# A two-block transformer kernel: where the modulation rows are placed in the first half

## The reference, cut to what matters

```python
mod = silu(c) @ w_ada[l] + b_ada[l]                 # 1024 x 6144
sh_m, sc_m, gt_m, sh_f, sc_f, gt_f = split(mod, 6)
h = rms_norm(x, g_pre_mix[l]) * (1 + sc_m) + sh_m
y = token_mixer(h, ...)                              # 3656 columns of w_in, attention, w_out
x = x + gt_m * rms_norm(y, g_post_mix[l])
h = rms_norm(x, g_pre_ffn[l]) * (1 + sc_f) + sh_f
y = (gelu(conv3(h @ w_up_act)) * (h @ w_up_lin)) @ w_down     # width 2816
x = x + gt_f * rms_norm(y, g_post_ffn[l])
```

## Time and profile before

| what | value |
|---|---|
| median of 3 runs | 2878.32 us (2877.91 to 2879.34) |
| the profiled execution | 2881.45 us, its span 2879.8 us |
| mean granted clock of TensorE | 0.937 of full speed |
| TensorE matmul busy | 2512.0 us (87%) |
| VectorE busy | 1790.6 us (62%) |
| ScalarE busy | 1218.0 us (42%) |
| GpSimd busy | 1000.2 us (35%) |
| bytes moved | 412.98 MB, 143 GB/s on average |
| first network (to the first block of columns of the second) | about 960 us |

### The profile page before, as it was taken

The page is one execution under the profiler, slowest core; times in us unless marked ns, Lnnn a source line. Parts: engine busy times, 40 slices in busy tenths (PEclk is TensorE's granted clock), DMA queues, the critical chain, the costliest instruction groups (busy, mean ns, idle before and its releaser), DMA issues. The chain is left out here.

```text
span 2879.8 us, 34433 instructions
## 1 busy us (share of the span) xinstructions
PE 2512.0 (87%) x12828; PEld 2073.3 (72%) x12828; DVE 1790.6 (62%) x2311; ACT 1218.0 (42%) x2102; POOL 1000.2 (35%) x827
## 2 busy tenths in 40 slices
PE   2986978986969799998775899999899997999898
PEld 2765976765867678886442778888788886777897
DVE  5777686875668687775997544454554534245554
ACT  3434444445555443445443433233433334234543
POOL 0111100113355687771554345443353421001221
PEclk9997999997989899999887999999899998999999
DMA  8445576443455355553100133344233332221452
GB/s 297 154 154 208 201 263 224 154 152 126 183 210 214 132 172 182 195 167 125 41 32 15 52 139 146 117 147 153 81 132 140 144 126 88 88 92 56 143 194 96
DMA packets 118294, 412.98 MB, mean 143 GB/s; under 512 B 13552, under 2 KB 17776, under 8 KB 118128
## 3 DMA queue, kind: packets, MB, share of 16 engines
q1 hardware_dynamic: 117152, 407.49, 40.5%
q10 hardware_dynamic: 976, 3.29, 0.3%
HBM read 409.68 MB, written 1.05 MB: 143 GB/s over the span
## 5 line engine op out<-in xcount | busy, mean ns | idle before, releaser
L1581 DVE TENSOR_TENSOR sl<-raw,sh 128x1024 fp32r<-128x1024 f32 x534 | 757.0, 1441 | 518.6 <-ACT sh L1272 518.3
L1006 PE MATMUL ps<-hH,sh 128*128 128x256 f32 (+1 forms) x2496 | 844.0, 338 | 81.3 <-DVE hL L1667 61.8
L1007 PE MATMUL ps<-hL,sh 128*128 128x256 f32 (+1 forms) x2496 | 838.1, 336 | 0.0
L1008 PE MATMUL ps<-hH,sl 128*128 128x256 f32 (+1 forms) x2496 | 837.4, 336 | 0.0
L1272 ACT ACTIVATE sh<-raw 128x1024 fp32r<-128x1024 f32 x534 | 539.5, 1036 | 341.0 <-PE ps L1008 300.7
L1006 PEld LDWEIGHTS ps<-hH,sh 128*128 128x128 f32 x2496 | 484.4, 194 | 139.8 <-issue 52.4
L1007 PEld LDWEIGHTS ps<-hL,sh 128*128 128x128 f32 x2496 | 483.4, 194 | 51.9 <-issue 1.0
L1008 PEld LDWEIGHTS ps<-hH,sl 128*128 128x128 f32 x2496 | 483.3, 194 | 51.4
L2054 POOL TENSOR_TENSOR raw<-raw,cB 128x1024 f32<-128x1024 f32 x144 | 375.8, 2610 | 185.3 <-DVE V L1593 182.9
L1593 DVE CUSTOM_DVE_ANT_0 mjunk<-raw,cB,V 128x1024 bf16<-128x1024 f32 x240 | 382.0, 1592 | 31.8 <-DMA V<-in_vec 16.4
L2125 POOL TENSOR_TENSOR uLl<-F,uHh 128x256 fp32r<-128x256 f32 (+1 forms) x132 | 156.7, 1187 | 565.7 <-ACT uHh L1468 442.5
(11 more groups left out here) (183 smaller groups left out, 2719.8 us busy)
## 6 DMA issues: line engine op xcount, KB each, us to landing
raw<-in_w SPq DMA_DIRECT2D x756, 512.0 KB, 4.3
raw<-in_w SPq DMA_DIRECT2D x16, 256.0 KB, 3.1
cB<-in_rpb SPq DMA_DIRECT2D x64, 64.0 KB, 2.6
X<-in_x ACTq DMA_DIRECT2D x1, 1024.0 KB, 12.1
X<-in_ctx ACTq DMA_DIRECT2D x1, 1024.0 KB, 18.5
out<-X SPq DMA_DIRECT2D x2, 512.0 KB, 3.1
raw<-in_w SPq DMA_DIRECT2D x2, 288.0 KB, 4.6
cB<-in_c ACTq DMA_DIRECT2D x1, 512.0 KB, 6.0
```

The source lines that it names most:

```text
L1006: self.e.matmul(out, lh, rh, start=start, stop=False)
L1007: self.e.matmul(out, lh, rl, start=False, stop=False)
L1008: return self.e.matmul(out, ll, rh, start=False, stop=stop)
L1581: self.e.tensor_tensor(lo[:, 0:w], raw[:, 0:w], hi[:, 0:w].bitcast(F32), ALU.subtract).then_inc(self.sems["w_lo"], 1)
```

## The change

Six edits. The rates of the first network's stages are new: more blocks in the projections and up products, none in attention, output and down products. FIRST (14) goes, and 8 blocks are placed ahead of the first norms. In `ffn1` the coefficients (with `before_x`, so also the context norms) are made after block of columns 18 of layer 0 and 14 of layer 1, no longer after the last. The load of V moves from ScalarE's queue to the head of SP's, the load of the context from ScalarE's queue to SP's `ctx_vec`, and ScalarE's order becomes c, x, C.

```diff
--- before.py
+++ after.py
@@ -28,9 +28,8 @@
 SPL = 6
 AHEAD = 6
 TAIL = 3
-RATES = {"proj": 0.25, "att": 1.0, "out": 0.5, "up0": 0.25, "down0": 0.75, "up1": 0.25, "down1": 0.5, "ffn2": 1.0,
+RATES = {"proj": 0.8, "att": 0.0, "out": 0.0, "up0": 0.56, "down0": 0.0, "up1": 0.7, "down1": 0.0, "ffn2": 1.0,
          "conv": 0.0, "late": 0.5}
-FIRST = 14
 OWE = 3
 NBANK = 8
 
@@ -551,9 +550,11 @@
             self.add("glu1", l=l, c=c, ba=ba, bu=bu, s=s, f=f, fid=fid, u=self.u_at)
             self.left(ba, bu)
             self.pace(2)
+            if c == (18, 14)[l]:
+                self.flush()
+                AB = [ab_next()]
         self.flush()
         self.rate = RATES[f"down{l}"]
-        AB = [ab_next()]
         hid = self.new()
         st2 = {}
         self.down(("w_down", l), ("u1", fid), KF, 0, [0, 1],
@@ -769,7 +770,7 @@
         AB = []
         h = self.new()
         firsts = []
-        self.fill(FIRST)
+        self.fill(8)
         for t in range(2):
             self.norm_tile(h, t, AB, 0, None, t == 1)
             firsts.append(self.firsts.pop())
@@ -944,6 +945,7 @@
                           bias_load=self.bias_load, final=self.final_out)
 
     def start(self, s):
+        self.e.dma_start(self.m["V"][:, :], self.dram["vec"]).then_inc(self.sems["ld1"], 16)
         self.next = 0
         for _ in range(RAW):
             self.issue()
@@ -963,6 +965,8 @@
         self.issue()
 
     def ctx_vec(self, s):
+        self.e.dma_start(self.m["X"][:, 2:4, :], self.dram["ctx"].rearrange("b (t p) d -> p (b t) d", p=P)).then_inc(
+            self.sems["ld3"], 16)
         self.mods("w_ada", 1, 5, 1)
         for k, n in enumerate(("c2", "cc")):
             src = bass.AP(tensor=self.dram[n].tensor, offset=0, ap=[[0, P], [1, D]])
@@ -1248,11 +1252,11 @@
 
     def start(self, s):
         m, dram = self.m, self.dram
-        loads = [(m["C"][:, :], dram["cst"]), (m["V"][:, :], dram["vec"]),
+        loads = [(m["C"][:, :], dram["cst"]), None,
                  (m["X"][:, 0:2, :], dram["x"].rearrange("b (t p) d -> p (b t) d", p=P)),
-                 (m["X"][:, 2:4, :], dram["ctx"].rearrange("b (t p) d -> p (b t) d", p=P)),
+                 None,
                  (m["cB"][:, 0, :], bass.AP(tensor=dram["c"].tensor, offset=0, ap=[[0, P], [1, D]]))]
-        for k in (4, 0, 2, 1, 3):
+        for k in (4, 2, 0):
             self.e.dma_start(*loads[k]).then_inc(self.sems[f"ld{k}"], 16)
         self.wait_ge(self.got("start_ones"))
         self.e.activation(m["ones"][:, :], m["F"][0][:, 0:P], ACT.Copy).then_inc(self.sems["a_sb"], 1)
```

## The result

The changed kernel takes 2899.4 us (median of 4 runs, 2896.62 to 2900.06) where the kernel before takes 2878.83 (4 runs, 2877.91 to 2883.51): a ratio of 1.0068, 95% interval 1.0052 to 1.0083. It is slower by 20.6 us, 0.7%. The profiled execution took 2898.99 us, its span 2897.0, 17.2 more than the span before; the mean granted clock is 0.937 in both.

A forecast was written before the change was run, and what follows sets the result against it. TensorE bounds most projections; in the up stages no engine is full, VectorE's chain with ScalarE sets the pace. Terms summed to +14: 2895 for the profiled execution, 2892 for the median; range 2855 to 2920, likeliest case 2880 to 2905.

The forecast's parts named there:

- Start, -4: Before the first projections: with V loaded first, modulation blocks M begin near 13.8 and coefficients come at 44.6; gain 4 us.
- Projections, +14: Projections of both layers: the extra modulation blocks M are only partly covered and cost 7 us a layer.
- Attention and output 0, -10: Layer 0's attention and output: the 14 modulation blocks M there leave; gain 10 us, bounds 5 and 18.
- Layer 1, -8: Layer 1's attention and output: 7 modulation blocks M leave, the wait for activation vectors only moves; gain 8 us.
- the third rival: Before layer 1's up stage: output matmuls do not cover the 14 us vector wait; +8, 2900; chance within the forecast's 0.45.
- Up 0, -1, and the gap behind, -10: Layer 0's up stage: 15 more modulation blocks for -1 us; before its down stage, no forced blocks, gain 10 us.
- Up 1, +38: Layer 1's up stage: VectorE and GpSimd stand for each other, 8.8 us a block of columns for 6.8; +38 us.
- I take 8.8, between them: Layer 1's up stage: the time per block of columns, chosen between a low end of 8.4 and a high end of 9.6.
- the first rival: Layer 1's up stage: every multiply stands in VectorE's way, +53 for +38, context squares and scales +8; 2915; chance 0.16.
- Context norms, +5, and the gap, -10: Context norms: +17 in layer 1's up loop, -12 at its down stage; empty TensorE before down and first splits: -10.
- Hidden: Layer 1's up stage: each multiply ends before the next split is ready, +7 in place of +38; 2857; chance 0.29.
- Nothing: Whole kernel: the modulation blocks M leave chains that others of like length replace; 2878; chance 0.1.

The follow-up runs named there:

- Experiment seven: Changed kernel with the old rates of projections, attention and output (0.25, 1.0 and 0.5): 2895.93 us.
- experiment six: Changed kernel with the context and its activation vectors loaded at the start of layer 1's attention: 2891.06 us.
- experiment eight: Changed kernel with only layer 0's coefficients moved back behind the last block of its up stage: 2901.31 us.
- Experiments two: Changed kernel with only layer 1's coefficients and context norms moved back behind the last block of its up stage: 2895.92 us.
- three: Changed kernel with GpSimd's multiply cut to 8 columns in 30 modulation blocks of layer 1's up stage (result not the reference's): 2859.96 us.
- eleven: The kernel of nine with the rates of layer 1's up and down stage at 0.50 and 0.25: 2868.56 us.
- nine: Changed kernel with layer 1's old up and down rates, old place of its coefficients and context norms, and early context loads: 2858.18 us.
- ten: The kernel of nine with the rate of layer 1's up stage at 0.36 instead of 0.25: 2859.16 us.

## Why the prediction was right in sign and size

The forecast was 2892.0 and the likeliest case's own range 2880 to 2905; 2899.4 lies in it, 7.4 above. Its reason, VectorE and GpSimd in turns in up 1, is what the runs show. Of the 7.4, 3.2 are the sum of the terms below; most of the rest is the 3.1 us that the forecast took off because the profiled execution before lay that much over its median. The changed kernel's lies 0.4 under its own.

**Start, -4: right** (-4.8; coefficients at 43.74 for a predicted 44.6).

**Projections, +14: right** (+14.9). Experiment seven confirms the cause.

**Attention and output 0, -10: right** (-12.9), by the M that left. **Layer 1, -8: too much** (-2.8). The step that failed is "I take the wait as moved, not removed": ScalarE's wait grew to 9.39 us and the 11 us of output matmuls did not cover it. That is the third rival, "the activation vectors", with the price there of 8 us: the early load shortened the stretch by 10.1 us and the whole by 8.3. A second thing was in no term: GpSimd's norm steps behind a multiply, some 2 us (experiment six).

**Up 0, -1, and the gap behind, -10: right** (+0.7 and -12.3), with blocks of columns of 5.83 us for a predicted 5.68. That the coefficients' new place mattered was wrong: once no block is forced, it is worth nothing (experiment eight). **Down 0, "its 14 blocks leave without a gain": wrong** by 4.3 us: the down stage went from 62.8 to 60.4 and its tail from 14.5 to 12.6.

**Up 1, +38: right in mechanism, too small.** The mis-sized term is "I take 8.8, between them". The high end, orders written out with every multiply in the way, had 8.5, 9.3, 10.6, 9.3 and 10.4; measured were 8.0, 9.36, 10.49, 9.36, 10.22. Without the norms' 13.8 the stage grew by 47.8. So the likeliest value was one end, not the middle: the first rival's first half (+53) was nearer.

**Context norms, +5, and the gap, -10: right.** 13.8 us in the loop (+17 forecast), -24.3 in gap and down 1 (-22). The rival's further 8 us for squares and scales did not come.

The misses nearly cancel: +9.8 in up 1's M, +5.2 in layer 1's output and +3.1 in small ones, against -4.3 in down 0, -2.9 and -2.3 in layer 0's stretches, and -3.2 and -2.3 in the norms and in down 1. That the sum of +14 came so near the measured +17.2 is in part luck, since the main term was further off.

**The other rivals.** "Hidden" is refuted: the stage grew by 61.6 us and splits behind an M took 3.0 us for 1.2, since an M was followed at once by a split or an M. "Nothing" (2878) is refuted by the ratio's interval.

## What to carry to other kernels

Two engines whose instructions stand for each other, as VectorE's splits and M and GpSimd's multiplies do here, are close to one engine for the planner: add their times, and write the order out instruction by instruction; where that gives a number, take it rather than a middle between it and a bound. Before handing an operation to a second engine, ask what it would cost on the first (here 1.28 us there, against up to 2.2 us of standing). With 1.4 M a block of columns the first engine alone was faster (9.07 us for 9.49), with 0.72 neither was (7.44 and 7.36). Work forced at a stage's end is paid by TensorE, but spreading it is free only where the loop has room: in layer 0 it took away a gap of 12.3 us for 0.7 in the loop, in layer 1 one of 18.4 for 15.5. And place a load that replaces a buffer a stage ahead of its first reader.

## What was not expected

- Splitting one GpSimd instruction in two made the changed kernel 14.5 us faster: VectorE gets its turn after half the time.
- Without GpSimd in it, VectorE's double product cost 9.07 us a block of columns for the 9.49 of the shared one, with 1.2 us more of its own work per M.
- The second projections and attention (460 to 640 us) run at a granted clock of 0.91 in some executions and 0.87 or 0.88 in others of the same steps, and last 182 or 185 to 186 us. A difference of 4 us there in single profiles is no effect of an edit. Experiments two, three, six and eight to eleven have the lower clock in their profiles. All four that ran on one of the chips (two, eight, nine, ten) do, but on each of the two other chips both values occur. What sets it was not tried.
